# Stick-breaking attention: later heads' projections at steps 3, 13, 24, 34 and 43, an earlier weight split, and memory-attention rows in four places

## What is computed

```python
h = _rmsnorm(x, g_pre[layer])
proj = h @ w_in[layer]
# stick-breaking, 8 heads of 64, per block of 128 queries
z = jnp.einsum('bqhd,bkhd->bhqk', qb, k).astype(jnp.float32) * scale
log_1mb = jnp.where(strict, jax.nn.log_sigmoid(-z), 0.0)
between = lax.cumsum(log_1mb, axis=3, reverse=True) - log_1mb
w = jnp.where(strict, jnp.exp(jax.nn.log_sigmoid(z) + between), 0.0)
return jnp.einsum('bhqk,bkhd->bqhd', w.astype(v.dtype), v)
# memory attention, 4 heads of 64 over 256 memory rows
sc = jnp.einsum('bshd,bmhd->bhsm', mq, mkv[:, :, 0]).astype(jnp.float32) * MEM_HEAD_DIM ** -0.5
pm = jax.nn.softmax(sc, axis=-1).astype(mkv.dtype)
y_m = jnp.einsum('bhsm,bmhd->bshd', pm, mkv[:, :, 1]).reshape(b, s_len, MEM_WIDTH) * jax.nn.silu(m_g)
```

## Time and profile before

| | us |
|---|---|
| median of 3 runs | 2110.27 |
| lowest, highest | 2102.15, 2114.96 |
| the profiled execution | 2109.54 |
| its span in the profile | 2107.7 |
| share of the span: PE busy | 90% |
| DVE busy, ACT busy, POOL busy | 64%, 52%, 26% |
| mean granted TensorE clock | 0.928 of full speed |

### The profile page before, as it was taken

The page is one execution under the profiler, slowest core; times in us unless marked ns, Lnnn a source line. Parts: engine busy times, 40 slices in busy tenths (PEclk is TensorE's granted clock), DMA queues, the critical chain, the costliest instruction groups (busy, mean ns, idle before and its releaser), DMA issues.

```text
span 2107.7 us, 34253 instructions
## 1 busy us (share of the span) xinstructions
PE 1895.4 (90%) x11552; PEld 1604.3 (76%) x11552; DVE 1346.4 (64%) x2805; ACT 1087.5 (52%) x2406; POOL 557.1 (26%) x438
## 2 busy tenths in 40 slices
PE   6999998899999999999999689998688889888998
PEld 6999997777877777777777577776466656667886
DVE  7606886576767676767676724444578888864544
ACT  6421111566666665656665523343477878872221
POOL 0000000344444443434343400102143444440000
PEclk9999998899999898989898869998689999989999
DMA  6322132001010101010100112425502122024542
GB/s 219 100 65 65 65 104 70 6 7 25 5 25 5 25 5 25 5 25 6 25 12 19 46 60 63 144 81 139 115 6 70 38 60 54 6 85 156 191 148 80
DMA packets 121867, 129.29 MB, mean 61 GB/s; under 512 B 81936, under 2 KB 94992, under 8 KB 120464
## 3 DMA queue, kind: packets, MB, share of 16 engines
q1 hardware_dynamic: 121744, 127.86, 20.9%
HBM read 85.89 MB, written 41.94 MB: 61 GB/s over the span
## 4 chain that ended last, share of the span: by engine, by line
PE 68%; DVE 15%; ACT 8%; issue 7%; DMA 2%; POOL 1%; SPq 0%; DVEq 0%; ACTq 0%; POOLq 0%
PE ps L658 6%; PE ps L612 6%; PE ps L613 5%; PE ps L614 5%; PE ps L644 4%; PE ps L599 4%; PE ps L601 4%; PE ps L600 4%; DVE small L1499 4%; PE ps L843 3%; PE ps L892 3%; PE ps L893 3%; PE ps L894 3%; PE ps L632 3%; PE ps L801 2%
## 5 line engine op out<-in xcount | busy, mean ns | idle before, releaser
L1639 POOL TENSOR_TENSOR ring_r<-ring,sp_hi 128x512 fp32r<-128x512 f32 (+1 forms) x320 | 358.8, 1121 | 833.2 <-DVE sp_hi L1362 833.2
L658 PEld LDWEIGHTS ps<-v,ring 128*128 128x128 f32 x2176 | 303.8, 202 | 37.3 <-issue 13.3
L658 PE MATMUL ps<-v,ring 128*128 128x65 f32 x2176 | 299.8, 280 | 4.9 <-ACT ring L1017 3.3
L1005 ACT ACTIVATE ring<-ps 128x512 f32<-128x512 f32 (+1 forms) x320 | 170.3, 532 | 250.2 <-PE ps L633 188.9
L1665 POOL TENSOR_TENSOR p<-p 128x1024 f32<-128x1024 f32 (+4 forms) x96 | 170.5, 1788 | 258.4 <-ACT p L1152 258.4
L612 PE MATMUL ps<-ht_hi,w_hl 128*128 128x512 f32 x448 | 202.5, 452 | 15.6 <-DVE sb_s L1389 7.9
L599 PE MATMUL ps<-w_hl,ht_hi 128*128 128x256 f32 x768 | 213.5, 278 | 0.7 <-DVE w_hl L1240 0.6
L600 PE MATMUL ps<-w_hl,ht_hi 128*128 128x256 f32 x768 | 213.3, 278 | 0.0
L601 PE MATMUL ps<-w_hl,ht_lo 128*128 128x256 f32 x768 | 213.2, 278 | 0.0
L1359 DVE SCALAR_TENSOR_TENSOR ring<-ring,ps 128x512 f32<-128x512 f32 (+1 forms) x320 | 191.7, 599 | 29.1 <-ACT ring L1010 28.1
L1376 DVE SCALAR_TENSOR_TENSOR acc<-ps,acc 128x256 f32<-128x256 f32 (+3 forms) x288 | 108.6, 377 | 138.7 <-PE ps L658 131.0
(11 more groups left out here) (185 smaller groups left out, 4010.6 us busy)
## 6 DMA issues: line engine op xcount, KB each, us to landing
w_raw<-in_w_narrow SPq DMA_DIRECT2D x18, 512.0 KB, 4.1
xb<-in_x SPq DMA_DIRECT2D x16, 512.0 KB, 3.9
gate_scr<-ring SPq DMA_DIRECT2D x64, 128.0 KB, 1.8
qk_scr<-w_hl SPq DMA_DIRECT2D x32, 256.0 KB, 3.4
gb<-gate_scr SPq DMA_DIRECT2D x16, 512.0 KB, 3.7
yb<-y_scr SPq DMA_DIRECT2D x16, 512.0 KB, 4.7
xr<-in_x SPq DMA_DIRECT2D x16, 512.0 KB, 4.2
out_y<-ob SPq DMA_DIRECT2D x16, 512.0 KB, 2.9
```

The source lines that it names most:

```text
L658: mm = pe.matmul(ps[:, 4 + i % 2, j * (HD + 1):(j + 1) * (HD + 1)], ring[:, 4 + i % 2, j * P:(j + 1) * P], v1[:, kb, :], start=True, stop= ...
L1639: nc.gpsimd.tensor_tensor(ring_r[:, i % 4, j0 * P:], ring[:, i % 4, j0 * P:], sp_hi[:, i % 4, j0 * P:].bitcast(F32), ALU.subtract).then_in ...
```

## The change

The projections of a head start at slots 3, 13, 24, 34 and 43 in place of 5, 14, 28 and 36. The entry at 43 is the same projection as the entry at 3, for the next head: slots 43 and 44 of one head are slots 3 and 4 of the next, so its first two parts run in the trailing slots of one loop pass and the last two in slots 5 and 6 of the next. A head still has four projections. The weight split starts at slot 16 in place of 20. The memory rows go to four places of `acc` in place of two, with a semaphore for each.

```diff
 SB_LEAD = 5
-SB_PROJECT = ((0, 2, 5), (0, 3, 14), (1, 0, 28), (1, 1, 36))
-SB_SPLIT = 20
+SB_PROJECT = ((0, 2, 3), (0, 3, 13), (1, 0, 24), (1, 1, 34), (1, 2, 43))
+SB_SPLIT = 16
...
+        def m_rows(k):
+            return acc[:, k % 2, k // 2 % 2 * 2:k // 2 % 2 * 2 + 2, :]
...
-        m_yout = [sem("m_yout0"), sem("m_yout1")]
+        m_yout = [sem(f"m_yout{u}") for u in range(4)]
...
                     sp.dma_start(y_scr[qb * P:(qb + 1) * P, c0:c0 + 2 * HD].rearrange("p (a d) -> p a d", a=2),
-                                 acc[:, i % 2, 0:2, :]).then_inc(m_yout[i % 2], 16)
+                                 m_rows(i)).then_inc(m_yout[i % 4], 16)
...
                     for q in range(2):
                         sp.wait_ge(sb_yout[q], 1 + 16 * SB_H * NT // 2)
-                        sp.wait_ge(m_yout[q], 16 * N_MT // 2)
+                        for u in (q, q + 2):
+                            sp.wait_ge(m_yout[u], 16 * N_MT // 4)
...
-                    if k >= 2:
-                        dve.wait_ge(m_yout[k % 2], 16 * (k // 2))
+                    if k >= 4:
+                        dve.wait_ge(m_yout[k % 4], 16 * (k // 4))
...
-                    nc.vector.tensor_tensor(acc[:, k % 2, 0:2, :],
+                    nc.vector.tensor_tensor(m_rows(k),
...
-            for q in range(2):
-                dve.wait_ge(m_yout[q], 16 * N_MT // 2)
+            for u in range(4):
+                dve.wait_ge(m_yout[u], 16 * N_MT // 4)
```

## The result

The changed kernel takes 2092.75 us (median of 14 runs, 2082.58 to 2102.12), the kernel before 2115.03 (14 runs on the same chips). The ratio is 0.989, 95% interval 0.988 to 0.991: 1.1% faster, some 22 us. The forecast was 2039.5 with a range of 2012 to 2078, so the direction was right and the size wrong by a factor of three.

A forecast was written before the change was run, and what follows sets the result against it. PE was taken to bound stick-breaking, losing time to idle gaps and to running at 1.2 GHz. Gains of 27 us idle, 35 clock and 8 memory sum to 70, so 2109.5 - 70 = 2039.5 us, range 2012 to 2078.

The forecast's parts named there:

- the three waits for L1389: Stick-breaking: PE's waits of 2.45, 0.24 and 0.63 us for DVE's low projection parts should all go, 3.32 us a head.
- the moved weight load: Stick-breaking: SP's weight load, issued in slot 5, lands in 4.1 us, well before slot 16; no cost.
- The memory term: End of memory attention: four places let step 28 go ahead, step 30 waits for step 26's store; 8 us, ends 3 and 9.
- the signs: What would show the forecast right, including gaps in slots 21 to 23 with POOL as releaser and DVE over 90% busy.
- The idle step: Stick-breaking heads: PE's idle falls from 7.2 to 3.6 us a head, 27 us over 7.5 heads.
- slots 28 to 33: Stick-breaking: two low pieces against full steps leave PE idle for 0.3 us, from 0 to 0.6.
- slots 7 to 12: Stick-breaking, no projection: DVE's 1.46 us of low pieces becomes a debt; 0.2 us of PE idle, between 0 and 0.98.
- Slots 17 to 23: Stick-breaking: DVE's low parts and weight pieces fall due earlier; 2.4 us of PE idle, ends 1.8 and 2.9.
- The clock step: Stick-breaking: of 49 us recoverable from low clock, 14 stay for a 6.83 us stretch every second head; 35 us gained.
- A: Stick-breaking: other gaps keep the clock low as long as today; only idle and memory gains come, 2074.5 us; chance 0.22.
- B: Stick-breaking slots 17 to 23: DVE's larger debt limits idle gain to 11 us, clock drops as often; 2090.5 us, chance 0.08.
- Its sign: PE idle of over 5 us in slots 20 to 24 would show that B holds.

The follow-up runs named there:

- the rows alone: Kernel before with only the memory rows in four places, projections and split as before: ratio 0.996 to the kernel before.
- Short low parts: Changed kernel with DVE forming 2 of the 512 columns of each low part of a projection in stick-breaking: 2069.1 us, one execution.
- short moves: Changed kernel with ACT moving out 2 of the 512 columns of each projection in stick-breaking: 2060.3 us, one execution.
- the kernel with moved weight pieces: Changed kernel with the eight weight pieces in pairs beside the projection parts, from slot 14: ratio 0.982 to the kernel before.
- short sums: Changed kernel with DVE's output sums of steps 14 to 17 over 2 of 64 columns per head block: 2059.6 us, one execution.
- the schedule alone: Kernel before with only the new projection places and the split at slot 16, memory rows in two places: ratio 0.996 to the kernel before.
- all shifted: The fastest kernel with every projection a slot or so earlier, the next head's first at slots 20 to 23: ratio 0.976 to the kernel before.
- the fastest kernel: Changed kernel with the next head's first projection in slots 21 to 24, two others shifted, weight pieces paired: 2050.1 us, 0.971 to the kernel before.

## Why the prediction was wrong

**What held.** PE sets the pace; the three waits for L1389 went from the loop (one of 2.07 us came at slot 3 of the first head, ahead of the loop); projection work is neither added nor removed; the moved weight load cost nothing; no stretch at slot 3 or step 12 was left in the middle heads. The memory term was sound: 8 us forecast, with step 30 waiting for about 4 us; 8.0 and 4.16 in the rows alone, and 22.3 to 23.2 us from step 25 to the last in eight of the ten profiles with four places. In the other two, the changed kernel's among them, it was 25.5, with the instruction of 6.1 us. Of the signs, POOL stood as releaser at the gaps, but DVE was busy for 82% of the time ahead of the drop and not over 90% (ACT for 90%).

**The idle step failed: "Together 3.6 us of idle a head against 7.2".** It was 7.05. Two terms were mis-sized, and both came out beyond the ends that I gave them. For slots 28 to 33 I wrote 0.3 "with 0.63 as the most seen"; the gaps there are 0.38, 0.83 and 0.61 us. Before, the projection at 36 came four slots after the moves at 32 and took the rest of the debt before it showed; now six bare slots follow. For slots 7 to 12 I wrote 0.2, and 0.63 + 0.70 us came, in slots 8 and 11. The prediction had the reason in hand: a full slot costs DVE 1.85 us against 1.82 on PE, so a bare slot cannot pay back anything, and the 1.46 us of low parts must surface as idle if enough bare slots follow. It was then not applied; and ACT's three moves, 1.8 us in the same slots, were left out of the sum. Short low parts returned 1.9 us a head, short moves 3.3. Slots 17 to 23 (2.4 forecast) had 0.26 + 0.25 + 0.90 + 0.34 + 0.95 = 2.7, as far as that was right. Over the stage 63.8 us of idle became 56.3: 7.5 returned, not 27.

**The clock step failed: "I allow one stretch of 6.83 us at 3.4 us in every second head".** The place was right, slots 21 to 23; what came was 10.24 us or more in every head. PE was busy for 81.1 us of the low stretches of the eight heads, half of which is 40.6, where 14 were allowed; before it was 108.2, or 54.1. The rows had said that 0.98 and 0.83 us "only just left the clock alone", and the forecast made them larger: that is a case for a stretch in every head, not in half of them. And heads are not independent draws. In the kernel with moved weight pieces every head from the third on met the stretch at the same slot. Nor is one head's stretch enough to bring on the next: with short sums the first head had it and the following six did not.

**A cost that the sum left out: the start behind a gap.** The heads gave 11.9 us, while 7.5 of idle and 54.1 - 40.6 = 13.5 of clock make 21. The traces show the rest. In a run of matmuls of 512 columns each adds 0.23 us to PE's busy time (from one start to the next); the first behind a gap adds its whole 0.50. Taken over all shapes, a matmul that starts behind a gap at the full clock adds 0.22 us more than the same matmul in a run, and gaps of 0.06 us have such a start too. A middle head had 8.8 such starts before, 1.9 us together, and has 14 now, 3.1 us. That is 1.15 us a head and 9 in all: 7.5 + 13.5 - 9 = 12. The run with short moves agrees: its middle heads have 9.2 such starts, 2.2 us together, and PE is busy for 1.3 us less in them than in the changed kernel, though no matmul was cut. So the change took out a few long gaps and put in more short ones, which cost PE nearly as much.

**Of the rivals,** A (2074.5) and B (2090.5) share the truth: the clock stayed low in part, and a debt of DVE (and of ACT, which B didn't name) took the place of the wait. B named the place of the low stretch and came within 1 us of the profiled execution, with a chance of 0.08. That nearness is in part luck: it allowed 11 us of idle saved, where 7.5 came, and nothing from the clock, where 13.5 came and 9 were lost to starts; and slots 17 to 23, where it saw the debt, had little more than I had counted. Its sign, over 5 us of idle in slots 20 to 24, did not come (2.4 us).

The Trainium skill ("TensorE: Matmul & The Clock Gate", HAM oscillation) counts half of the throttled time as the penalty. By it, as an estimate, a stretch of 10.24 us costs 5.12. The runs bear that out only in part. With short sums a head is 5.12 us shorter, but over the middle heads 0.6 of that is idle, which leaves 4.5, near the 4.6 of my count by busy time. A second stretch of 10.24 us within one kernel cost 3.64 us in the schedule alone, where PE's idle fell by 0.4 beside it, and 4.4 to 4.6 in all shifted (a head of 101.7 against 97.1 to 97.3). Stretches of 3.41 us in the fastest kernel cost 1.6 to 1.7 us, which is half.

**Open:** how the gaps of slots 21 and 22 divide between the latency of the chain and DVE's own work (1.48 us stayed with short sums), and what decides whether the clock falls behind them.

## What to carry to other kernels

Where an engine needs as long for a slot as the one that sets the pace (here 1.85 us against 1.82), every extra instruction on it is a debt that is paid only in slots in which the pacing engine has more to do; write it down for each stretch without such slots, for each engine that takes part, before moving anything. Fill the slots in which the pacing engine waits with work that it has to do anyway: here one projection moved by three slots gave more than the whole change. And price a gap on PE three times: for its length, for the start behind it (0.22 us here), and for the clock behind it (3.6 to 4.6 us for a stretch of 10.24). In a loop, don't count the last as a draw of its own in each pass.

## What the runs showed that was not expected

- The size of a gap does not tell whether the clock falls. With short low parts it fell after 0.25 and 0.91 us (716.41 and 718.86), with short sums it held through 0.42 and 1.06 us (719.66 and 722.74).
- The stretches can lock to the head: with one stretch of 10.24 us in each, six heads in a row took 102.28 to 102.43 us in the changed kernel, though low weight pieces of 2 columns (102.37) or pieces moved elsewhere (102.42) change the work in them. It is not a rule: the second stretch in the sixth head of the schedule alone did not return in the seventh, and the fastest kernel had one of 3.41 us in its fourth and sixth heads alone.
- A stretch at 1.2 GHz can last long under full load: 23.9 us in the last head of the kernel with all projections shifted, with PE on record as busy for all of it. Its busy time:

```profile
1110.70:1134.60 23.90, 23.89 (x90) 21.56 (x91) 15.71 (x38) 11.33 (x25) 9.87 (x9) 0.50 0.03 6
```

- Two DVE instructions over two columns are on record for 2.7 and 1.8 us, in some executions for 6.1 and 5.2, at the moment SP begins thirteen loads; both end together. What holds them was not tried.
